# Eleven gathered rows of group A moved from the table stage to the first merge and the query projection of group B

## What is computed

```python
def block(args):
    hb, ib, gb = args
    a = jnp.einsum('nhkd,nd->nhk', u_tab[ib], hb)
    coef = (gb * jax.nn.gelu(a.astype(jnp.float32), approximate=False)).astype(hb.dtype)
    return jnp.einsum('nhk,nhkd->nd', coef, v_tab[ib])
...
x  = x + (sum_b sigmoid(gate_b(h)) * (branch_b @ w_br_b)) @ w_out
x  = x + PEER(RMSNorm(x))
```

## Time and profile before

| | us |
|---|---|
| median of 3 runs | 4558.77 |
| lowest, highest | 4558.13, 4562.73 |
| the profiled execution | 4560.95 |
| its span in the profile | 4559.2 |
| TensorE busy | 4049.4 (89%) |
| VectorE busy | 3104.3 (68%) |
| GpSimd busy | 1295.2 (28%) |
| bytes read and written | 1450 MB and 76 MB, 335 GB/s over the span |

### The profile page before, as it was taken

One profiled execution on the slowest core, in us unless ns is written; L12 is line 12 of the kernel. 1 busy time (PEld: TensorE's weight loads), 2 busy tenths in 40 slices (PEclk: granted clock), 3 DMA queues, 4 the chain that ended last, 5 costly groups with the idle time before them and its releaser, 6 DMA issues.

```text
span 4559.2 us, 60824 instructions
## 1 busy us (share of the span) xinstructions
PE 4049.4 (89%) x23368; PEld 3503.4 (77%) x23368; DVE 3104.3 (68%) x4561; ACT 924.5 (20%) x1339; POOL 1295.2 (28%) x822
## 2 busy tenths in 40 slices
PE   7999999999899989999798989999999997676565
PEld 7999999999789987888687878887787775343221
DVE  7444344444647567888687885888898656788766
ACT  4334434323433421011001000000000004000100
POOL 0000000000000013435442432444444321667664
PEclk9999999999899999999899999999999998787777
DMA  6555677775365569999999999999999996999998
GB/s 219 198 207 191 212 287 288 282 261 188 108 238 204 200 234 422 413 403 414 415 406 373 404 423 408 405 423 424 423 413 423 424 403 280 413 390 401 422 422 353
DMA packets 303267, 1529.03 MB, mean 335 GB/s; under 512 B 36394, under 2 KB 108538, under 8 KB 134948
## 3 DMA queue, kind: packets, MB, share of 16 engines
q0 software_dynamic: 114288, 830.54, 44.0%
q1 hardware_dynamic: 188772, 695.78, 40.3%
HBM read 1450.06 MB, written 76.13 MB: 335 GB/s over the span
## 4 chain that ended last, share of the span: by engine, by line
PE 55%; DMA 27%; DVE 8%; issue 4%; DVEq 3%; ACT 2%; POOL 2%; ACTq 0%; SPq 0%; POOLq 0%
PE psum L588 27%; PE psum L654 11%; DMA sb_raw_u<-in_wstream 10%; PE psum L3343 9%; DMA sb_ring<-in_peer_v,sb_idx_all 8%; DMA sb_raw<-in_wstream 6%; PE psum L3604 2%; DVE sb_acc_b L3500 2%; POOL sb_ring L3153 2%; PE psum L2342 2%; DVEq L2371 1%; DVE sb_split L572 1%; DVE sb_acc L3179 1%; DVE sb_ring L3174 1%; ACT sb_split L568 1%
## 5 line engine op out<-in xcount | busy, mean ns | idle before, releaser
L588 PE MATMUL psum<-sb_actr,sb_split 128*128 128x264 f32 x7344 | 912.3, 286 | 28.1 <-DVE sb_split L572 14.3
L588 PEld LDWEIGHTS psum<-sb_actr,sb_split 128*128 128x128 f32 x7344 | 902.1, 190 | 32.7 <-issue 19.7
L572 DVE TENSOR_TENSOR sb_split<-sb_raw,sb_split 128x2048 fp32r<-128x2048 f32 x201 | 460.5, 2291 | 625.0 <-ACT sb_split L568 624.4
L3061 POOL DMA_INDIRECT sb_ring<-in_peer_u,sb_idx_all x256 | 417.2, 1630 | 1100.3 <-PE psum L588 522.7
L3179 DVE SCALAR_TENSOR_TENSOR sb_acc<-sb_ring,sb_coef,sb_acc 128x2048 f32<-128x2048 f32 x256 | 601.8, 2351 | 162.0 <-DMA sb_ring<-in_peer_v,sb_idx_all 147.2
L3174 DVE CUSTOM_DVE_ANT_0 sb_ring<-sb_ring,sb_htok 128x2048 f32<-128x2048 f32 x264 | 595.5, 2290 | 157.6 <-DMA sb_ring<-in_peer_u,sb_idx_all 127.6
L3061 POOL DMA_INDIRECT sb_ring<-in_peer_v,sb_idx_all x256 | 403.9, 1578 | 655.0 <-DVE sb_acc L3179 577.5
L3604 PE MATMUL psum<-sb_ring,sb_diag 128*128 128x512 f32 x512 | 353.7, 854 | 241.2 <-DMA sb_ring<-in_peer_v,sb_idx_all 234.0
L3500 DVE SCALAR_TENSOR_TENSOR sb_acc_b<-sb_ring,sb_coef_b,sb_acc_b 128x2048 f32<-128x2048 f32 x192 | 451.4, 2351 | 127.2 <-DMA sb_ring<-in_peer_v,sb_idx_all 113.9
L3153 POOL DMA_INDIRECT sb_ring<-in_peer_v,sb_idx_all x256 | 442.3, 1728 | 247.8 <-DVE sb_acc_b L3500 124.3
L3343 PE MATMUL psum<-sb_h2b,sb_raw 128*128 128x256 f32 x2048 | 457.9, 383 | 25.5 <-DMA sb_raw<-in_wstream 25.5
(11 more groups left out here) (455 smaller groups left out, 4351.0 us busy)
## 6 DMA issues: line engine op xcount, KB each, us to landing
sb_raw<-in_wstream SPq DMA_DIRECT2D x398, 1024.0 KB, 7.6
sb_raw_u<-in_wstream SPq DMA_DIRECT2D x64, 1024.0 KB, 23.0
sb_states<-in_state SPq DMA_DIRECT2D x32, 512.0 KB, 3.9
sb_states_t<-in_stateT SPq DMA_DIRECT2D x32, 512.0 KB, 4.4
out_gla_s<-sb_states SPq DMA_DIRECT2D x32, 512.0 KB, 3.0
dram_z<-sb_zst SPq DMA_DIRECT2D x121, 132.0 KB, 3.7
dram_z_b<-sb_zst SPq DMA_DIRECT2D x65, 128.0 KB, 1.8
sb_vrow<-dram_v SPq DMA_DIRECT2D x8, 1024.0 KB, 5.6
```

What stands on the lines that cost most here:

```text
L572: nc.vector.tensor_tensor(split[:, slot, 1, :], raw[:, slot, :], split[:, slot, 0, :], ALU.subtract).then_inc(lo_ready, 1)
L588: last = nc.tensor.matmul(psum[:, bank, 0:ntok], w[a], acts(b, kt), start=(i == 0 and a == 0 and b == 0), stop=(i == len(kts) - 1 and a == 1))
L3061: nc.gpsimd.indirect_dma_start(ring[g % RING][:], None, ins[table], bass.IndirectOffsetOnAxis(ap=col, axis=0)) \
```

## The change

Two lists of numbers change; the sum of rows is the same.

```diff
@@ dve_out_b
             dve.drain().then_inc(normed, 1)
-            beside(27)
+            beside(31)
@@ block.vector
             dve_project_b(dve, beside)
-            dve_merge_b(dve, N_BA, N_BC, beside, lambda k: 4 if k in (1, 3, 5, 7) else 3 if k < GATES_B else (2, 1, 1, 0)[k - GATES_B])
+            dve_merge_b(dve, N_BA, N_BC, beside, lambda k: (3, 7, 3, 6, 3, 4, 3, 4, 3, 3, 3, 3, 2, 1, 2, 1)[k])
```

## The result

| | before | changed |
|---|---|---|
| median of 20 runs, us | 4558.77 | 4566.10 |
| lowest, highest | 4552.50, 4566.51 | 4559.69, 4573.47 |
| span of the profiled execution | 4559.2 | 4564.0 |

The ratio changed to before is 1.0018, 95% interval 1.0012 to 1.0024: the change costs 5 to 11 us, where the prediction had -14.3. (The medians differ by 7.3 us, the two profiled executions by 4.8.) The forecast of 4544.5 us and its range up to 4561 both missed.

The account below looks back on a forecast made before the run. The prediction took the table to run at DMA's pace, 424 GB/s when full. Terms -23.3 + 6 + 2 + 1 = -14.3 us, from the profiled 4560.95 us and 2.2 lower for the median, gave 4544.5 us; range 4536 to 4561.

Parts of the forecast that it names:

- What bounds the kernel: Whole kernel: one stream of transfers, full at 424 GB/s, sets the table's pace; each row taken out saves 2.47 us.
- Part 3: Attention and following merges: a head moves into the attention, adding 9.36 us there, and the merges return 7.4; net +2 us.
- Part 4: TensorE's clock: drops after longer waits in the attention and at the merge's end; +1 us, bounds 0 and 4.
- Part 2: First merge: seven rows more, partly filling DMA's room, delay its last multiply to 2430.7 us; +6 us, bounds 3 and 17.3.
- Part 1: Table: 11 rows less save 27.2 us, of which 3.9 come back at its start; -23.3 us.
- from there: Table: VectorE has caught up after 25 blocks, and afterwards a block costs 7.2 us.
- Part 5: Query projection: four rows more at its end cost TensorE 0; VectorE's first table head starts some 3 us later.
- blocks at 7.57 us to the end: Table: sign that the prediction is wrong, if blocks stay at 7.57 us to the end.
- The first merge giving back what the table gains: Rival: all 17.3 us of row transfers land on the first merge's end; -2.5 us, 4556 us; chance 0.24.
- The one slower rival: Rival: rows stay behind through the table, so blocks stay at 7.57 us; +14 us, 4573 us; chance 0.07.

Follow-up runs that it names:

- e9: The changed kernel with the loads of B's stored gates one output later in SyncE's order; 4572.79 us, 1.0031 of before.
- e13: The changed kernel with the loads of stored gates 34 to 47 issued by ScalarE instead of SyncE; 4568.45 us, 1.0023 of before.
- e17: The kernel before with only its sixth head moved, from row 62 in the second merge to row 55 in the attention; 4565.17 us, 1.0017 of before.
- e6: The kernel before with no row moved, its heads before the outputs where they stand in the changed kernel; 4577.08 us, 1.0036 of before.
- e5: The changed kernel, all eleven rows moved, with heads kept before the same outputs as in the kernel before; 4554.32 us, 0.9992 of before.
- e2: The kernel before with only the seven rows more in the first merge; 4571.40 us, 1.0035 of before.
- e1: The kernel before with only four rows more in the query projection (31 instead of 27); 4552.87 us, 0.9991 of before.
- e16: The kernel before with only eight rows more in the query projection (35 instead of 27); 4562.92 us, 1.0004 of before.
- e18: The kernel before with seven rows more in the first merge and heads kept at their outputs; 4561.80 us, 1.0012 of before.
- e7: e5 with its last head in the output projection instead of the third merge; 4564.18 us, 1.0010 of before.
- e8: e1 with its last head in the output projection, at row 98 instead of 82; 4559.44 us, 1.0004 of before.
- e14: e1 with the loads of gates 34 to 47 issued by ScalarE; 4555.68 us, 0.9990 of before.

## Why the prediction was wrong

**What bounds the kernel** held as far as the runs show: over the six stages DMA moves 97% of what 424 GB/s would (1515.2 of 1559.9 us), and e9 and e13, which took away one wait each, only put another in its place. What was missing is the other side, that a new order can make DMA stand.

**Part 3 is the step that failed**, "Net +2". "The whole 9.36 adds to it" came true (9.9). "VectorE has no waits there ... 6.9 us fall away for certain" did not: I took VectorE as the merges' limit because it hardly waits in them (3.8 us, for TensorE), and looked at 4.70 us of TensorE's. e17 has the step alone: +10.0 and -3.3 instead of +9.4 and -7.4. The 4.70 us did go there; what they were exchanged for is waits for weights. A block of VectorE's work taken out of a stage frees only as much as the transfers beside it can follow. The changed kernel does worse, +3.9, because its last head stands before the third merge's fourth output, not its eleventh, and e6 shows that the places without any row moved give +7.0. The output projection, "in the bound", took +5.6: TensorE's 512 records of it are 2.0 us longer (112.78 against 110.77), and its wait for VectorE behind them is 10.57 us instead of 6.95. The part's sum was +2 and came out at +19.4 (9.9, 3.9 and 5.6), of which the 2.0 are clock (part 4). That is 17.4 of the 19.1 us between the forecast -14.3 and the 4.8 between the spans. What is shown by an experiment of its own is the attention and the merges; why the output projection grew by its other 3.6 us is not: it is 131.6 to 131.8 us long in e6 (heads alone) and e5 (rows alone), and 135.9 with both in e2.

**Part 4**, the clock, was +1 with bounds 0 and 4, and 2.0 us can be read at the start of the output projection; its share in the attention is not separated. Behind the wait of 9.63 us the granted clock is 0.58, most of it the lower level of 1.2 GHz, and TensorE does 13 records in the time in which it did 22 before; from 2609 us on it is 1.00:

```profile
2604.20:2609.00 4.80, 4.80 (x13) 3.91 (x14) 4.51 (x3) 0.00 (x0) 1.18 (x1) 0.58 1.00 423
```

**Part 2** had the right size (+6, measured +7.0) by a wrong way. "TensorE's weights do not suffer", the rows pay: the last multiply at 2432.59 (forecast 2430.7) came right behind TensorE, which had waited 4.43 and 5.12 us for weights. SyncE issued the first stored gate, which waits for VectorE, at 2375.86 instead of 2362.35, and the weight block behind it 7.5 us later. SyncE's queue before, and in the changed kernel:

```profile
2362.35 0.33 SPq L2318 DMA_DIRECT2D sb_gt<-dram_z_b  x1
2368.74 0.33 SPq L638 DMA_DIRECT2D sb_raw<-in_wstream  x1
```

```profile
2355.67 7.23 SPq L638 DMA_DIRECT2D sb_raw<-in_wstream  x2
2375.86 0.33 SPq L2318 DMA_DIRECT2D sb_gt<-dram_z_b  x1
2376.23 0.91 SPq L638 DMA_DIRECT2D sb_raw<-in_wstream  x2
```

In e9 the rows paid and the length was the same: by bytes the term is independent of who waits. Five early rows are 12.4 us of DMA, less the 3.5 us of idle that they filled, 8.9; the merge is 7.0 longer. The two late rows, 4.9 us by bytes, cost 0.7. 2275 to 2300 us rose from 350 to 422 GB/s as foreseen; 2250 to 2275 stayed at 379.

**Part 1** was -23.3 and came out at -18.6. The seven early rows carry it: 13.7 us in e2 with 6.15 MB less, 2.0 us a row. The four of the query projection gave 2.6 us in e1's table (952.6 us), not 6. The 6.61 us of idle before the first head are gone, as foreseen. The cheaper blocks came too, but only in the middle of the table. From 3100 to 3500 us, in the kernel before and in the changed one:

```profile
3100.00:3500.00 400.00, 377.96 (x1702) 319.46 (x1701) 347.50 (x657) 31.40 (x114) 187.33 (x102) 1.00 1.01 420
```

```profile
3100.00:3500.00 400.00, 391.06 (x1790) 338.05 (x1790) 349.20 (x685) 32.97 (x120) 177.72 (x99) 1.00 1.01 418
```

With 32 records a block that is 7.5 us a block before and 7.15 in the changed kernel, the 7.2 of the prediction, and nearly three blocks more in the same time. From 3500 us on VectorE is behind again (up to 3800 it waits 89.2 us for rows of additions), and TensorE still stops before each block:

```profile
3787.38 7.17 PE L3343 MATMUL psum<-sb_h2b,sb_raw 128*128 128x256 f32 x32 [0.40 <-DMA sb_raw<-in_wstream]
3794.91 7.17 PE L3343 MATMUL psum<-sb_h2b,sb_raw 128*128 128x256 f32 x32 [0.36 <-DMA sb_raw<-in_wstream]
```

That is 7.53 us from one to the next. So the prediction's "from there" failed: VectorE does not stay caught up. That is not all of it, since blocks cost as much late in e16, where VectorE waits for the table's results and hardly for rows (VectorE's waits there from 3480 to 3800 us: in total, times, longest):

```profile
DVE sb_acc L3179 <- ACT sb_a_stage L3298: 65.9, 23, 5.2
DVE sb_acc L3179 <- DMA sb_ring<-in_peer_v,sb_idx_all: 18.3, 13, 2.9
```

Why a block does not get cheaper there is open. The prediction also overlooked a line of its own: in the earlier trace rows VectorE waits 12.2 us for the table's results, so even in the kernel before it was not behind throughout. I had named blocks at 7.57 us to the end as a sign that I am wrong; late blocks do stay at 7.5, and the gain was there all the same.

**Part 5** was 0 for the stage; it became 2.0 us shorter. **The rivals**: none was this. The first merge giving back what the table gains put the loss in a stage that took 7.0 us, not 17. The one slower rival (4573 us) had the direction, but it put the loss into the table, which did shorten.

**What stays open.** e5 and e18 differ by the four rows of the query projection and by 7.5 us, twice what the four gave alone in e1; and e7, e8 and e16 lost more than any theory had. The ledger shows the idle time, not which wait will make it.

**Faster than both.** e1 and e14 take 0.9991 and 0.9990 of the time before, 4 to 5 us, and e5 0.9992. All are 10 to 13 us below the changed kernel; only e14's interval excludes no difference from before, and just so, as one of several that were tried. So none of the three is shown to be faster than before. The smallest edit of them is the one number 31.
